# A hybrid decoder layer on Trainium2: preparing the next RWKV pair earlier within the substitution, and adding before gating in the FFN's tail

## The reference, cut to what matters

```python
def _rwkv7(p, prev_row, S0, P):
    ...
    w_log = -jax.nn.softplus(-(P['rwkv_w0'] + jnp.tanh(wd) @ P['rwkv_w_up'])) - 0.5
    decay = jnp.exp(-jnp.exp(w_log))
    a = jax.nn.sigmoid(P['rwkv_a0'] + ad @ P['rwkv_a_up'])
    kk = heads(kf * P['rwkv_k_k'])
    kk = kk / jnp.maximum(jnp.sqrt(jnp.sum(kk * kk, axis=-1, keepdims=True)), 1e-12)
    kf = heads(kf * (1.0 + (a - 1.0) * P['rwkv_k_a']))
    # for each token: S = S * w + (S @ -kk) (kk * a)^T + v k^T;  o = S @ r
    S_T, o = _wkv_scan(rf, decay, kf, vf, kk, a, S0)
    ...
    bonus = jnp.sum(rf * kf * P['rwkv_r_k'], axis=-1, keepdims=True) * vf

def _layer(...):
    ...
    ff, conv_T = _conv_ffn(h2, conv0, P)     # (silu(za) * zb) @ ffn_w_down
    x = x + g2 * _rmsnorm(ff, P['norm_post_ffn'])
```

## Time and profile before

| | us |
|---|---|
| three timed executions | 1659.0, 1670.96, 1673.98 |
| their median | 1670.96 |
| the profiled execution's own time | 1661.17 |
| its span, first to last instruction | 1659.0 |

### The profile page before, as it was taken

One profiled execution on the slowest core, in us unless ns is written; L12 is line 12 of the kernel. 1 busy time (PEld: TensorE's weight loads), 2 busy tenths in 40 slices (PEclk: granted clock), 3 DMA queues, 4 the chain that ended last, 5 costly groups with the idle time before them and its releaser, 6 DMA issues.

```text
span 1659.0 us, 28738 instructions
## 1 busy us (share of the span) xinstructions
PE 1431.8 (86%) x12458; PEld 1332.1 (80%) x12458; DVE 834.9 (50%) x1052; ACT 544.1 (33%) x715; POOL 115.0 (7%) x183
## 2 busy tenths in 40 slices
PE   4799998777477786779749999999999999999994
PEld 1799998444366675469728999999999999999994
DVE  3743333663655567361186545545445454454557
ACT  3311211555355531332244231322323223132234
POOL 0000000000212220112121000000000000000013
PEclk7899999898699997689979999999999999999997
DMA  8341111441000010112122111111111111111122
GB/s 343 109 115 52 39 51 40 165 168 65 1 3 3 3 37 24 57 39 115 38 115 83 50 53 49 42 46 38 63 38 51 38 38 63 38 51 39 42 86 103
DMA packets 36280, 107.60 MB, mean 65 GB/s; under 512 B 5640, under 2 KB 14616, under 8 KB 35280
## 3 DMA queue, kind: packets, MB, share of 16 engines
q1 hardware_dynamic: 36192, 106.30, 18.5%
HBM read 93.29 MB, written 11.40 MB: 63 GB/s over the span
## 4 chain that ended last, share of the span: by engine, by line
PE 72%; DVE 16%; ACT 6%; issue 3%; DMA 2%; SPq 1%; DVEq 0%; ACTq 0%
PE ps L513 48%; PE ps L918 11%; PE ps L667 4%; DMA raw<-ada 2%; DVE Z L1916 2%; PE ps L645 2%; PE ps L560 1%; DVE S L1571 1%; PE ps L589 1%; DVE mx L1573 1%; DVE acc L1950 1%; PE ps L494 1%; DVE ps L2027 1%; PE ps L768 1%; DVE acc L2028 1%
## 5 line engine op out<-in xcount | busy, mean ns | idle before, releaser
L513 PE MATMUL ps<-XS,spl 128*128 128x344 f32 x5112 | 813.1, 321 | 38.1 <-DVE XS L1879 20.6
L513 PEld LDWEIGHTS ps<-XS,spl 128*128 128x128 f32 x5112 | 808.7, 189 | 41.4 <-issue 25.2
L918 PE MATMUL ps<-act,spl 128*128 128x344 f32 x1440 | 230.8, 320 | 0.8
L918 PEld LDWEIGHTS ps<-act,spl 128*128 128x128 f32 x1440 | 226.9, 188 | 3.3 <-DVE acc L1950 3.3
L1916 DVE SCALAR_TENSOR_TENSOR Z<-U,par,Z 128x1023 f32<-128x1023 f32 x86 | 110.3, 1283 | 154.9 <-ACT Z L1298 149.4
L1280 ACT ACTIVATE spl<-raw 128x1024 fp32r<-128x1024 f32 x66 | 68.4, 1054 | 284.1 <-PE ps L918 198.4
L1950 DVE TENSOR_TENSOR acc<-acc,ps 128x1032 f32<-128x1032 f32 x80 | 98.4, 1230 | 112.0 <-PE ps L918 111.9
L1504 DVE TENSOR_TENSOR spl<-raw,spl 128x1024 fp32r<-128x1024 f32 x28 | 34.2, 1225 | 170.8 <-ACT spl L1018 170.8
L1869 DVE TENSOR_TENSOR spl<-raw,spl 128x1024 fp32r<-128x1024 f32 x66 | 79.6, 1222 | 61.3 <-ACT spl L1280 60.1
L1018 ACT ACTIVATE spl<-raw 128x1024 fp32r<-128x1024 f32 x28 | 29.6, 1060 | 211.0 <-PE ps L513 211.0
L1295 ACT ACTIVATE U<-ps 128x1032 f32<-128x1032 f32 x43 | 44.3, 1029 | 152.0 <-PE ps L513 150.3
(11 more groups left out here) (301 smaller groups left out, 1610.6 us busy)
## 6 DMA issues: line engine op xcount, KB each, us to landing
raw<-ada SPq DMA_DIRECT2D x48, 512.0 KB, 5.1
raw<-up SPq DMA_DIRECT2D x44, 512.0 KB, 3.5
raw<-down SPq DMA_DIRECT2D x22, 512.0 KB, 3.8
raw<-w_in SPq DMA_DIRECT2D x20, 512.0 KB, 3.6
xT<-xT SPq DMA_DIRECT2D x4, 1032.0 KB, 11.8
X<-xT SPq DMA_DIRECT2D x1, 4128.0 KB, 12.9
x_dram<-X SPq DMA_DIRECT2D x8, 516.0 KB, 2.6
o_y<-acc SPq DMA_DIRECT2D x24, 172.0 KB, 1.8
```

Of the source, the lines that this page charges most:

```text
L513: mm = nc.tensor.matmul(ps[:, 3 * bank_set + t, 0:SL], w[:, a, k * P:(k + 1) * P], x[:, k, b, t * SL:(t + 1) * SL], start=(k == order[0] a ...
L918: mm = nc.tensor.matmul(ps[:, 3 * (y % 2) + t, 0:SL], w[:, a, k * P:(k + 1) * P], act2[:, f, b, t * SL:(t + 1) * SL], start=(f == 0 and n ...
```

## The change

In the pairs: the list has the pieces in another order. Both halves of `turn` and the solve come before chain 4. The next pair's decay comes behind chain 4, rate ahead of p2a, norm ahead of p2b. `norm` is cut in two: its product stays `norm`, its Relu and Ln are the new piece `floor`, ahead of chain 10; `root` comes before the spread instead of between the two X evictions; `scan` follows X, kf and rkk lie between J1 and J2's outer step, kk and bonus behind J3. `exps` is cut in two as well: the exponential into R is the new piece `expr`, ahead of J3, and alpha and POOL's whole_decay wait for it alone; the other two exponentials stay `exps`, now behind Q.

In the tail: the third third is gated behind the eighth addition; ACT's copy of its high part follows the eighth square. `tail_total` and `tail_root` come two rows of features earlier. A table of rows (`NORMS_AFTER`) says after which addition which normalisation is done. For 13 of the 24 results the addition of the residual is done by POOL: DVE then forms the product in place. A one-column Ln after the fifth square of each third makes ACT load its table ahead of the root. The squares' places in `Z` and `U` are given by a table, since a third of `Z` and `U` is still wanted for the gating.

```diff
@@ order
-            pieces = [("p1a", 0), ("p1a", 1), ("chain", 0), ("p1a", 2), ("low", 0), ("chain", 1), ("p1a", 3), ("chain", 2),
-                      ("nbt", 0), ("values", 0), ("chain", 3), ("low", 1), ("values", 1), ("turn", 0), ("chain", 4),
-                      ("p1b", 0), ("p0", 0), ("chain", 5), ("turn", 1), ("solve", 0), ("nbt", 1), ("chain", 6), ("p1b", 1),
-                      ("p0", 1), ("chain", 7), ("decay", 0), ("p2a", 0), ("p2a", 1), ("chain", 8), ("mnk", 0), ("p2a", 2),
-                      ("p2a", 3), ("chain", 9), ("mnk", 1), ("rate", 0), ("p2b", 0), ("chain", 10), ("p2b", 1), ("scan", 0),
-                      ("chain", 11), ("W1", 0), ("W1", 1), ("norm", 0), ("kf", 0), ("chain", 12), ("spread", 0), ("chain", 13),
-                      ("X", 0), ("root", 0), ("X", 1), ("chain", 14), ("rkk", 0), ("J1", 0), ("chain", 15), ("J1", 1),
-                      ("outer", 0), ("kk", 0), ("J2", 0), ("bonus", 0), ("J2", 1), ("outer", 1), ("J3", 0), ("J3", 1),
-                      ("exps", 0), ("Q", 0), ("Q", 1), ("Q", 2), ("Q", 3), ("alpha", 0), ("kappa", 0), ("EO", 0), ("EO", 1),
-                      ("EO", 2), ("beta", 0), ("EO", 3), ("ends", 0), ("AR", 0), ("AR", 1), ("AR", 2), ("AR", 3)]
+                      ("nbt", 0), ("values", 0), ("chain", 3), ("low", 1), ("values", 1), ("turn", 0), ("turn", 1),
+                      ("solve", 0), ("chain", 4), ("decay", 0), ("p1b", 0), ("p0", 0), ("nbt", 1), ("chain", 5), ("p1b", 1),
+                      ("p0", 1), ("chain", 6), ("rate", 0), ("p2a", 0), ("p2a", 1), ("chain", 7), ("mnk", 0), ("p2a", 2),
+                      ("p2a", 3), ("chain", 8), ("mnk", 1), ("norm", 0), ("p2b", 0), ("chain", 9), ("p2b", 1), ("floor", 0),
+                      ("chain", 10), ("W1", 0), ("W1", 1), ("root", 0), ("chain", 11), ("spread", 0), ("chain", 12), ("X", 0),
+                      ("X", 1), ("scan", 0), ("chain", 13), ("J1", 0), ("chain", 14), ("J1", 1), ("kf", 0), ("chain", 15),
+                      ("J2", 0), ("rkk", 0), ("outer", 0), ("J2", 1), ("outer", 1), ("expr", 0), ("J3", 0), ("J3", 1),
+                      ("kk", 0), ("bonus", 0), ("Q", 0), ("Q", 1), ("Q", 2), ("Q", 3), ("exps", 0), ("alpha", 0), ("kappa", 0),
+                      ("EO", 0), ("EO", 1), ("EO", 2), ("beta", 0), ("EO", 3), ("ends", 0), ("AR", 0), ("AR", 1), ("AR", 2),
+                      ("AR", 3)]
@@ ACT, piece_of
+                elif piece == "expr":
+                    act.wait_ge(*nth("scan", j + 1))
+                    if j >= 2:
+                        act.wait_ge(s("outer_mm"), 2 * j - 2)
+                    nc.scalar.activation(R[par].rearrange("p u c -> p (u c)"), F0[:, 0:T], ACT.Exp, scale=-KAPPA
+                                         ).then_inc(signal("exp_r"), 1)
@@ the tail: tables
+        NORMS_AFTER = {(1, 3): [(0, 0)], (1, 4): [(0, 1)], (1, 5): [(0, 2)], (1, 6): [(0, 3)], (1, 7): [(0, 4)], (2, 0): [(0, 5)],
+                       (2, 1): [(0, 6)], (2, 2): [(0, 7)], (2, 3): [(1, 0)], (2, 4): [(1, 1)], (2, 5): [(1, 2)],
+                       (2, 7): [(1, k) for k in range(3, KD)] + [(2, k) for k in range(KD)]}
+        def sums_on_pool(t, k):
+            return k < 5 if t == 2 else k % 2 == 1
@@ the tail: PE and ACT
-                if t >= 1 and k == 3:
+                if t >= 1 and k == 1:
                     tail_total(t - 1)
...
+                if n == KD - 1:
+                    tail_hi(2)
+                if k == 4:
+                    nc.scalar.activation(eps[:, 4 + t % 2:5 + t % 2], eps[:, 0:1], ACT.Ln)
-                if t >= 1 and k == 3:
+                if t >= 1 and k == 1:
                     tail_root(t - 1)
@@ the tail: POOL
+            def tail_y(t, k):
+                w = min(SL, T - t * SL)
+                y = acc[:, k, t * SL:t * SL + w]
+                pool.wait_ge(s("y_scaled"), sums_before(t, k, True) + 1)
+                nc.gpsimd.tensor_tensor(y, y, x1_of(t)[:, k, 0:w], ALU.add).then_inc(s("y_summed"), 1)
             for t, k in TAIL:
                 if k < KD - 1:
                     tail_sum(t, k)
+                for x in NORMS_AFTER.get((t, k), ()):
+                    if sums_on_pool(*x) and x[0] == 0:
+                        tail_y(*x)
+            for t, k in TAIL[KD:]:
+                if sums_on_pool(t, k):
+                    tail_y(t, k)
@@ the tail: DVE
+                if sums_on_pool(t, k):
+                    nc.vector.scalar_tensor_tensor(y, y, gate[:, 1, k, 0:1], ps[:, 6 + t % 2, 0:w], ALU.mult, ALU.mult
+                                                   ).then_inc(s("y_scaled"), 1)
...
+            for t in range(2):
+                tail_gate(t)
+                tail_low(t)
...
+            for t, k in TAIL:
+                tail_add(t, k)
+                if (t, k) == (0, KD - 1):
+                    tail_gate(2)
+                elif (t, k) == (1, 0):
+                    tail_low(2)
+                for x in NORMS_AFTER.get((t, k), ()):
+                    tail_norm(*x)
```

More of the change, by code:

```diff
@@ L254, in build_program @@
         SAMPLE_STEPS = 9
-        PREP = ("decay", "rate", "norm", "root", "kf", "rkk", "kk", "bonus", "scan", "exps", "alpha", "kappa", "beta",
+        PREP = ("decay", "rate", "norm", "floor", "root", "kf", "rkk", "kk", "bonus", "scan", "expr", "exps", "alpha", "kappa", "beta",
                 "ends")
@@ L266, in order @@
             if j < 0:
[L267 to L268 removed]
+                return [("decay", 0), ("sample", 0), ("rate", 0), ("sample", 1), ("norm", 0), ("floor", 0), ("root", 0), ("sample", 2), ("kf", 0),
+                        ("rkk", 0), ("sample", 3), ("kk", 0), ("bonus", 0), ("sample", 4), ("scan", 0), ("expr", 0), ("exps", 0),
                         ("alpha", 0), ("kappa", 0), ("beta", 0), ("ends", 0)]
             pieces = [("p1a", 0), ("p1a", 1), ("chain", 0), ("p1a", 2), ("low", 0), ("chain", 1), ("p1a", 3), ("chain", 2),
[L271 to L275 removed]
[4 rows of a table removed]
+                      ("nbt", 0), ("values", 0), ("chain", 3), ("low", 1), ("values", 1), ("turn", 0), ("turn", 1),
[3 more added lines that the diff above has]
+                      ("chain", 10), ("W1", 0), ("W1", 1), ("root", 0), ("chain", 11), ("spread", 0), ("chain", 12), ("X", 0),
[5 rows of a table added]
             of_chain = ("chain", "outer")
@@ L290, in order @@
                     if x[0] in PREP:
-                        if x[0] not in ("decay", "rate", "scan", "bonus", "norm", "root"):
+                        if x[0] not in ("decay", "rate", "scan", "bonus", "norm", "floor", "root", "expr"):
                             out.append(("update", n))
@@ L313, in build_program @@
             "prep_mm": {"decay": ["p_decay"], "rate": ["p_rate"], "norm": ["p_norm"], "bonus": ["p_bonus"]},
-            "prep_act": {"decay": ["sig_decay"], "rate": ["sig_rate", "k_square", "k_rate"], "norm": ["k_floor", "k_log"], "root": ["k_norm"],
+            "prep_act": {"decay": ["sig_decay"], "rate": ["sig_rate", "k_square", "k_rate"], "floor": ["k_floor", "k_log"], "root": ["k_norm"], "expr": ["exp_r"],
                          "exps": ["exps"]},
@@ L474, in _ @@
             for n, (t, k) in enumerate(TAIL):
-                sp.wait_ge(s("y_ready"), n + 1)
+                if sums_on_pool(t, k):
+                    sp.wait_ge(s("y_summed"), sums_before(t, k, True) + 1)
+                else:
+                    sp.wait_ge(s("y_ready"), sums_before(t, k, False) + 1)
                 dma(io["o_y"][:, k, THIRDS[t]], acc[:, k, THIRDS[t]], s("y_out"))
@@ L954, in tail_total @@
                 if t == 2:
-                    pe.wait_ge(s("y_ready"), KD)
+                    pe.wait_ge(s("y_ready"), sums_before(1, 0, False))
+                    pe.wait_ge(s("y_scaled"), sums_before(1, 0, True))
                 nc.tensor.matmul(ps[:, 6 + t % 2, 0:SL], ones, sqF[:, THIRDS[t]], start=True, stop=False)
@@ L1138, in piece_of @@
                                          ).then_inc(signal("k_rate"), 1)
-                elif piece == "norm":
+                elif piece == "floor":
                     act.wait_ge(*nth("p_norm", j + 1))
@@ L1342, in _, with tail_hi @@
             act.wait_ge(s("g_done"), FC)
+            def tail_hi(t):
+                act.wait_ge(s("g_third"), t + 1)
+                nc.scalar.activation(act2[:, 1, 0, THIRDS[t]], G[:, THIRDS[t]], ACT.Copy).then_inc(s("hi_third"), 1)
             for t in range(3):
@@ L1351, in _ @@
                                      scale=col(PARAM_AT["ffn_conv_w"][0] + 2 * 2 * FC, 2 * FC - 1)).then_inc(s("third_out"), 1)
-                act.wait_ge(s("g_third"), t + 1)
-                nc.scalar.activation(act2[:, 1, 0, THIRDS[t]], G[:, THIRDS[t]], ACT.Copy).then_inc(s("hi_third"), 1)
+                if t < 2:
+                    tail_hi(t)
             def tail_root(t):
@@ L1981, in _, with tail_gate @@
             z, u = Z[:, 1], U[:, 1]
-            for t in range(3):
+            def tail_gate(t):
```

43 lines of the change are left out of this document (17 added, 26 removed).

## The result

The kernel after took 1650.55 us in the median of ten executions (1649.71 to 1656.2), the kernel before 1670.29 (ten, 1659.0 to 1673.98). The ratio of the two means is 0.9896, 95% interval 0.9873 to 0.992: 1.0% faster, at the edge of the 1% within which the prediction put 0.67 of its chances. The profiled execution of after, the shortest of its ten, took 1649.71 us, 11.5 less than that of before; its span is 11.2 shorter than the 1659.0 of the earlier trace rows.

The account below looks back on a forecast made before the run. No engine's sum bounds the second pair; a chain through several engines does. Pairs 5.8 plus tail 6.8 gave 12.6 us: 1648.6 from the profiled 1661.17, 1655.1 from base 1667.7; range 1641 to 1666.

Parts of the forecast that it names:

- the base: Starting time for the forecast: 1667.7 us, between the profiled 1661.17 and the median 1670.96, the median weighed by two thirds.
- Start of the first pair: Ahead of the first pair: alpha and whole_decay wait for the first exponential alone, so alpha starts 1.05 us earlier.
- First pair: First of four pairs: no chain there, the same steps as in the second give 1.0 us.
- Second pair: X starts 4.3 us earlier; DVE's later work at the pair's end leaves 1.2, with bounds of 0 and 4.3.
- Third pair: Third of four pairs: the same gain as in the second, 1.2 us.
- Fourth pair: X starts 5.7 us earlier, but six update steps stand ahead of AR: 1.35 gained, bounds 0 and 4.
- Tail: Last stage: earlier additions and normalising, 13 of 24 additions on POOL; gains about 6.8 us, bounds 3 and 9.5.
- the drain: Skill page's about 1.38 us per table switch, ahead of the spread in the pairs: total 1663.4; given no chance of its own.
- Rival 1: In the pairs DVE's end is not the bound; X's whole 4.3 passes in three pairs: 22 us, 1645.6; chance 0.26.
- Rival 2: DVE and POOL get in each other's way in pairs and tail: 7 us are left, 1660.7; chance 0.18.
- Rival 3: TensorE at its lower level in the pairs' decay, rate and norm: 1.8 us a product, all nine 1671.3; chance 0.04.

## Why the prediction was right, and where not

The time lies 4.6 us below the forecast and within the range. By the medians the gain was 19.7, 7.1 more than the 12.6 forecast, and the base 1670.3, 2.6 more than the 1667.7. On the two profiled executions the span gained 11.2, and there the steps missed to both sides: that their sum is so near 12.6 is in part luck. Step by step:

- *Start of the first pair*, 1.05 forecast: 1.04. Alpha started 0.43 earlier though the code ahead, the same in both, was 0.61 late.
- *First pair*, 1.0 forecast: 1.5.
- *Second pair*: X 4.3 earlier forecast, 4.6 measured; next p1a 1.2 forecast, 2.3 measured. Alpha took 1.20 and kappa waited for the exponentials, both as forecast. From Q to the next p1a it was 10.8 us, 11.0 forecast. X to Q was 15.1, 15.6 forecast, but only because two items in it were wrong and cancelled. "The root between the two X evictions goes (2.3)": with the root put back X to Q is 15.2, so there its move gave 0.1, and cost 2.4 ahead of the spread. And the bonus product (2.0) is no new cost "where it lay beside J2": in before it held J2's second half, which could only start when it was over (531.55 and 2.00 us):

```profile
533.48 1.15 PE L667 MATMUL ps<-LT,MP 64*64 64x64 f32 x32
```

With the root between the evictions in both orders X to Q grew from 13.9 to 15.2, by 1.3, where kf, rkk and bonus less the hidden part had been put at 4.0.

- *Third pair*, 1.2 forecast: 0.6. The same order would have gained as in the second; but p1b ran at a clock of 0.55, and decay to rate took 5.96 us instead of the second pair's 4.42 (4.42 in the third pair, too, in the run with the exponentials ahead of Q).
- *Fourth pair*, 1.35 forecast: 1.0 lost. X came 5.0 earlier (5.7 forecast) and the six steps stood ahead of AR as described; but behind PE's stands for the steps J2's second half, the second outer step and J3 ran at the lower clock: 1.40, 1.97 and 3.44 us, against 1.10, 1.15 and 2.03 in the run without the early Ln. There the same order gained 1.3, near the 1.35 forecast. (X was at the lower clock in before, too, 3.68 us against 3.34, and is no part of the loss.) The replay of DVE's queue was right; the step that failed is PE's clock, which it left at one.
- *Tail*, 6.8 forecast: 7.1, and nearly every item: additions 3.6 earlier than in before, counted from the tail's start (3.5), normalising 4.6 (4.3), the last gating pair 2.25 against 1.19 for the second third, which had no sums of POOL beside it (+1.1; 0.9 forecast), DVE's stand for the last root 3.5 (about 3). The in-place product took 0.56 beside POOL's sums. Where the data were there, the table loads had 0.01 to 0.02 us between load and activation in every stage; the drain that the Trainium skill's page "ScalarE: Activation LUTs" (section "What ACT_TABLE_LOAD costs") adds shows nowhere here.
- *Rival 1* (4.3 passes in every pair) is refuted by kappa's 1.70 us wait, and by the run that took the wait away. *Rival 2* (lock of DVE and POOL) showed as +0.46 at kk beside whole_decay, 1.74 instead of 1.28, and +1.1 at the gating; too small to decide. *Rival 3* (the lower clock): decay, rate and norm of the pairs ran at full clock in after, in 1.97 to 2.00 us. The mechanism was there, but at p1b of the third pair and at J3 of the fourth.

For the total the step that failed is the base: "I can't tell which group the next runs join, so I weigh the median by two thirds". It takes the scatter of before's executions for something that the change leaves alone. The forecast against the profiled execution was 1648.6, and after lies at 1649.7 to 1652.0 in nine of ten. The long executions of before that were profiled had long first pairs, at the lower clock behind a stand of PE, and none of the ten profiles of the new order has one. On the two profiles the pairs gained 3.8 with their start; by the ratios it was 9.8. What of the new order does it, the decay product in the stand or another piece, was not tried by itself (in the run with decay behind p1b's first half it still lies ahead of the second half, and the first pair took 49.48); and a part of the scatter, 2 to 6 us ahead of the pairs, comes and goes in both orders.

## What to carry to other kernels

Where executions of one kernel fall into groups, profile one of each group before the gain is worked out: a change of order that fills a stand of TensorE may take away what makes the long executions long, and this gain is in no row of a short one. On a chain through several engines, ask of a moved step what it lies beside, before and after: in one pair the root cost 0.1 us beside X's products and 2.4 in front of them, and the bonus product, priced at 2.0 in its new place, had held another product as long in its old one. And where a queue is full up to the end of a stage, look for an idle stretch earlier in the stage whose data have landed; two update steps moved there gave 2.3 to 4.5 us, by the clock that J3 had without them.

## What the runs showed of the hardware

A lower granted clock isn't tied to one place: in the five profiles of the same pairs it lay at p1b of the third pair (beginning at 550 to 553 us), early in the fourth (at 605 to 608), or in both, and J3 of the fourth was at it or not; the sum of the four pairs lay between 207.8 and 211.1 us. Behind stands of 1.81, 1.92, 2.10 and 2.20 us at the same instruction of the old order the decay product took 2.00, 3.80, 3.80 and 3.80 us; but behind stands of 2.07 and 1.49 us in the fourth pair J3 was at a clock of 1.00, and at 0.55 behind 2.08 and 1.19. And in the run without the early Ln ScalarE loaded a table ahead of an activation that still waited for its data: 1631.88 to 1633.16, for an Ln that began at 1635.69.
